# Latent attention scores as row tiles of TensorE, with the projections made for a pair of heads

## Chip, cores, metric

One core of a Trainium2 chip (trn2). The metric is device time in microseconds of one execution of the whole kernel.

## The reference, cut to what matters

A two-layer encoder over 1024 tokens of width 1024, all in fp32. Layer 0 mixes tokens by dilated attention, layer 1 by latent attention with 8 heads; both add 4 heads of attention into a memory of 256 tokens, and end in a mixture of 32 experts. The change is in the latent attention of layer 1:

```python
q = (rms_norm(c_q) @ w_qb).reshape(S, 8, 64 + 32)        # c_q: (1024, 256)
q_nope, q_pe = q[..., :64], apply_rope(q[..., 64:])
kv = (rms_norm(c_kv) @ w_kvb).reshape(S, 8, 64 + 64)      # c_kv: (1024, 128)
k_nope, v = kv[..., :64], kv[..., 64:]
k_pe = apply_rope(k_rope)                                 # (1024, 32), one for all heads
s = (q_nope . k_nope + q_pe . k_pe) * 96 ** -0.5          # per head, 1024 x 1024
o = softmax(s) @ v
```

So a score is a dot product over 96 numbers: 64 unrotated ones and 32 rotated ones, whose key part is the same for every head.

## The kernel before, in words

Every engine has its own program, written out by hand, and semaphores tie them together. The stages stand in the same order on each: layer 0's projections and attentions, its output projection, routing and experts, then for layer 1 the latents, the latent attention, the memory attention, output projection, routing and experts. Weights of the experts stream through a ring of six buffers of 16 KB per partition; the latent attention keeps its queries, keys and weights in the same ring, so SP asks for the second layer's first expert weights only when the latent attention is over (`expert_phase`, line 597).

Latent attention works in 32 units: 4 pairs of heads times 8 tiles of 128 queries. Before it, `latent_projection` (line 1156) makes the values of all heads (`for_act`, copied out by ACT at line 1293), and DVE rotates the shared key part (`latent_norms`, line 1951) into rows 64 to 95 of each of four key buffers. The first two heads are projected ahead of the loop (`head_projection`, line 1176): per head two halves of 512 tokens for the queries, 96 output rows, two products over the 256 latents each, and two products for the keys, 64 output rows, the two halves side by side in the columns of the array. All of them go to bank 7. ACT copies the 64 unrotated rows (`head_copy`, line 1461), DVE rotates the other 32 in four operations (`head_rope`, line 1963, lines 1971 to 1977), and PE waits for both before it writes the bank again. The heads of the next pair are projected inside the loop, one piece per unit: pieces 0 and 1 are query halves, 2 is the key product, 3 only a copy; 8 pieces in the 8 units of a pair.

In the loop PE does, per unit u: scores of head 0 of unit u + 1 (line 1210, banks 0 and 1), the transposes of head 1's probabilities of unit u (`turn`, line 1219), the transpose of the reciprocals of the sums (line 1236), a piece of projection, scores of head 1 of unit u + 1 (banks 2 and 3), the values of unit u (line 1230, both heads side by side in the columns), and the transposes of head 0's probabilities of unit u + 1. A product over fp32 is two instructions on PE. DVE does the maximum over 1024 scores (line 1989), scales it (1991), copies half of the transposed probabilities (1996), makes reciprocals of the sums spread over 128 columns (2005), copies them when they are transposed (2010), rotates a projected half, and multiplies the output (2016). ACT does the exponentials (1482), the other half of the transposed probabilities (1489), and the copies of projections (1468).

The waits that order this: scores of head hd wait until the same head's exponential of the unit before is done, since they write its banks; the values wait for the transposed probabilities and for the copy of the reciprocals; the first scores of a pair wait for the pair's copies and ropes.

The weights of a head are loaded by SP in two small transfers (`head_weights`, line 665), the first two heads' early, the others' when the projections of earlier heads are done. The weights of the output projection, 3 MB, are asked for when the input projection of layer 1 has been read (line 676).

Memory attention, after it, already takes its scores with 64 rows of the array for each head (line 907), two heads at a time:

```python
rows = slice(DH * (h % 2), DH * (h % 2) + DH)
last = mm(ps[:, 2 * b + h % 2, ...], queries[rows, h // 2, ...], keys[rows, h // 2, ...])
```

The experts use the array in columns (line 1051): products for 32 tokens in four column quarters, for 64 tokens in two column halves.

## Time and profile before

| | |
|---|---|
| runs shown | 2440.29, 2444.55, 2451.59 us |
| median | 2444.55 us |
| profiled execution, its own time | 2438.25 us |
| its span, first to last instruction | 2436.1 us |
| instructions in it | 37961 |
| mean granted TensorE clock | 0.946 |

The span leaves 2.15 us of the profiled execution's time outside. Times in the rows are microseconds from the start of the span. Engines: PE is TensorE (PEld its weight loads), DVE is VectorE, ACT is ScalarE, POOL is GpSimd, SP issues DMAs. A matrix instruction is shown from its start to a modelled end, so the distance between two starts says what one costs in a stream. A granted clock of 1.00 is 2.4 GHz, and the other level is 1.2 GHz.

### The profile page before, as it was taken

What the parts mean: (1) busy time and instruction counts of PE and PEld (TensorE: products, weight loads), DVE (VectorE), ACT (ScalarE), POOL (GpSimd) and SP (SyncE); (2) the same over time, 40 slices, a digit from 0 to 9 for tenths busy, and PEclk for the clock granted to TensorE, in tenths of its full rate; (3) what the DMA queues carried; (4) which work ended last, traced back from release to release, by engine and by line L of the source; (5) the groups of instructions that cost most, each with busy time, mean ns of one, the idle gap of its engine ahead of it and who ended that gap; (6) DMA issues with size and microseconds to landing.
All of it is one profiled execution on the core that took longest, in us unless ns stands there. A gap on an engine that the chain in (4) does not pass through costs nothing. (4 is left out here: it accounts for less than half of the span.)

```text
span 2436.1 us, 37961 instructions
## 1 busy us (share of the span) xinstructions
PE 2222.6 (91%) x15351; PEld 1184.0 (49%) x15351; DVE 841.7 (35%) x1791; ACT 468.2 (19%) x943; POOL 343.0 (14%) x401
## 2 busy tenths in 40 slices
PE   8999998886999999998797999989689999999964
PEld 4665757553444444444443556665444444444422
DVE  2133324634121212122825767642422212121216
ACT  0030304221010101011333444431201101010011
POOL 0000000141111111131600000003211111111305
PEclk9999998987999999999897999999689999999997
DMA  9022104344999999997310000010469999999945
GB/s 352 1 76 98 40 1 142 141 184 165 396 391 388 394 386 389 389 387 274 119 52 7 3 5 1 1 70 35 200 224 395 388 400 384 386 378 391 375 158 207
DMA packets 98871, 534.47 MB, mean 219 GB/s; under 512 B 23040, under 2 KB 46880, under 8 KB 73824
## 3 DMA queue, kind: packets, MB, share of 16 engines
q1 hardware_dynamic: 80672, 491.28, 51.8%
q0 software_dynamic: 18112, 41.99, 4.8%
q8 instruction: 60, 0.98, 0.2%
q14 instruction: 27, 0.22, 0.0%
HBM read 510.16 MB, written 41.45 MB: 226 GB/s over the span
## 5 line engine op out<-in xcount | busy, mean ns | idle before, releaser
L825 PE MATMUL banks<-ring,arena 128*32 128x256 f32 (+3 forms) x9952 | 1303.4, 461 | 38.5 <-DMA ring<-in_exp_w_gu 15.0
L825 PEld LDWEIGHTS banks<-ring,arena 128*32 128x32 f32 (+2 forms) x9952 | 536.4, 124 | 746.3 <-issue 608.7
L825 PE MATMUL banks<-ring 128*128 128x512 f32 (+2 forms) x976 | 372.2, 531 | 10.7 <-ACT ring L1468 7.1
L825 PEld LDWEIGHTS banks<-ring 128*128 128x128 f32 (+1 forms) x976 | 183.9, 194 | 156.6 <-issue 139.8
L1830 DVE TENSOR_TENSOR arena<-arena,banks 128x384 f32<-128x384 f32 x65 | 36.0, 554 | 609.7 <-ACT arena L1392 609.7
L761 POOL DMA_INDIRECT expert_out<-arena,scatter_idx x64 | 61.1, 955 | 824.4 <-DVE arena L1839 804.4
L1392 ACT ACTIVATE arena<-banks 128x384 f32<-128x384 f32 x65 | 31.9, 490 | 735.8 <-PE banks L825 735.8
L825 PE MATMUL banks<-arena 128*64 128x128 f32 (+5 forms) x1664 | 157.8, 303 | 16.7 <-DMA arena<-in_mem_w_kv 9.6
L825 PEld LDWEIGHTS banks<-arena 128*64 128x64 f32 (+3 forms) x1664 | 139.0, 169 | 50.2 <-issue 38.0
L718 POOL TENSOR_TENSOR arena<-arena,ln_gb 128x1024 f32<-128x1024 f32 x28 | 69.5, 2482 | 626.5 <-ACT arena L1357 626.5
L1836 DVE COPY arena<-banks 32x256 f32<-32x256 f32 x132 | 56.2, 425 | 280.1 <-PE banks L825 279.2
L825 PE MATMUL banks<-arena,ring 128*128 128x256 f32 (+3 forms) x288 | 101.0, 529 | 13.6 <-DVE ring L1977 11.7
L1407 ACT COPY arena<-banks 32x256 f32<-32x256 f32 x128 | 46.2, 361 | 313.7 <-PE banks L825 313.0
L1600 DVE CUSTOM_DVE_ANT_0 arena<-banks,arena 128x256 f32<-128x256 f32 (+1 forms) x160 | 54.1, 394 | 148.8 <-PE banks L825 145.5
L1989 DVE TENSOR_REDUCE max_and_sum<-banks 128x1 f32<-128x1024 f32 x64 | 77.5, 1212 | 38.6 <-PE banks L825 38.2
L1482 ACT ACTIVATE arena<-banks,neg_max 128x1024 f32<-128x1024 f32 x64 | 71.3, 1114 | 91.7 <-DVE neg_max L1991 90.5
L1031 PEld LDWEIGHTS banks<-ident,arena 96*128 96x128 f32 x520 | 47.5, 146 | 66.3 <-issue 63.4
L1357 ACT ACTIVATE arena<-arena,ln_rstd 128x1024 f32<-128x1024 f32 x32 | 39.7, 1240 | 191.2 <-DVE ln_rstd L1683 191.2
L1031 PE MATMUL banks<-ident,arena 96*128 96x96 f32 x520 | 59.7, 260 | 16.6 <-issue 8.5
L825 PEld LDWEIGHTS banks<-arena,ring 128*128 128x128 f32 (+2 forms) x288 | 48.6, 183 | 51.7 <-issue 47.0
L720 POOL TENSOR_TENSOR arena<-arena,ln_gb 128x1024 f32<-128x1024 f32 x28 | 71.1, 2539 | 2.2
L1826 DVE COPY arena<-banks 128x768 f32<-128x768 f32 x65 | 62.3, 958 | 24.9 <-PE banks L1031 17.5
(176 smaller groups left out, 1575.7 us busy)
## 6 DMA issues: line engine op xcount, KB each, us to landing
ring<-in_exp_w_gu SPq DMA_DIRECT2D x130, 2048.0 KB, 17.2
ring<-in_exp_w_down SPq DMA_DIRECT2D x65, 2048.0 KB, 21.8
ring<-in_x_t SPq DMA_DIRECT2D x6, 2304.0 KB, 16.4
moe_in<-arena POOLq DMA_DIRECT2D x16, 512.0 KB, 3.0
arena<-expert_out SPq DMA_DIRECT2D x16, 512.0 KB, 4.3
ring<-expert_out SPq DMA_DIRECT2D x16, 512.0 KB, 4.4
ring<-in_a_w_in SPq DMA_DIRECT2D x6, 1024.0 KB, 17.3
arena<-in_a_w_in SPq DMA_DIRECT2D x4, 1024.0 KB, 14.0
```

The source lines that it names most:

```text
L718: nc.gpsimd.tensor_tensor(X[:, t], X[:, t], ln_gb[:, 0], ALU.mult).then_inc(gmul_done, 1)
L720: nc.gpsimd.tensor_tensor(X[:, t], X[:, t], ln_gb[:, 1], ALU.add).then_inc(x_ready, 1)
L761: pool.indirect_dma_start(y_d[l][:, :], bass.IndirectOffsetOnAxis(ap=s_idx[0:CAP, b:b + 1], axis=0), ys[0:CAP, b], None, bounds_check=2 * ...
L825: return nc.tensor.matmul(out, lhsT, rhs, start=start, stop=stop)
L1031: last = nc.tensor.transpose(ps[:, k // 4, (k % 4) * CAP:(k % 4 + 1) * CAP], xs[0:CAP, b, k * P:(k + 1) * P], ident[0:CAP, 0:CAP])
L1357: nc.scalar.activation(X[:, t], X[:, t], ACT.Identity, bias=rstd[:, t, 1:2], scale=rstd[:, t, 0:1]).then_inc(norm_done, 1)
L1407: nc.scalar.copy(ys[WIDE:CAP, b, g * 256:(g + 1) * 256], ps[NARROW * g:NARROW * g + NARROW, 7, 0:256])
L1482: nc.scalar.activation(prob[:, hd], ps[:, 2 * hd:2 * hd + 2].rearrange("p a b -> p (a b)"), ACT.Exp, bias=neg_max[:, hd, 0:1], scale=SCALE ...
L1600: last = nc.vector.tensor_tensor_reduce(out=prob[:, b, h * 256:h * 256 + w], in0=ps[:, 2 * b + h % 2, (h // 2) * 256:(h // 2) * 256 + w], ...
L1826: return V.tensor_copy(xs_t[b].rearrange("p (a c) n -> p a (c n)", a=2), ps[:, 0:2, 0:4 * CAP])
L1836: return V.tensor_copy(ys[WIDE:CAP, b, g * 256:(g + 1) * 256], ps[NARROW * g:NARROW * g + NARROW, 7, 0:256])
L1989: V.tensor_reduce(stat[:, hd, 0, 0:1], ps[:, 2 * hd:2 * hd + 2].rearrange("p a b -> p (a b)"), AX.X, ALU.max).then_inc(row_max, 1)
```

## The change

A product over 64 or 32 rows of the array leaves the other rows free, and a row tile is a product put on a part of the rows. The queries and keys are stored anew for that. `q_nope` and `k_nope` hold a pair of heads, one in partitions 0 to 63, one in 64 to 127. `q_rope` holds the rotated part of both heads of a pair, each twice, in four quarters of 32 partitions; `k_rope` holds the rotated key part in four quarters, keys 0 to 511 in the first and third, 512 to 1023 in the second and fourth. A unit's scores are then four products over 64 rows, alternating between the halves, and four over 32 rows, one in each quarter, that add to the same four banks. They are written for both heads at once, at the place of head 0's, and wait until both exponentials of the unit before are done.

The projections are made for the pair: six per pair instead of eight pieces per two heads, each 128 output rows wide (rotated queries, unrotated queries and keys, for each half of the tokens), ten products in all. The first pair's go to banks 0 to 5 without a wait between them, the later ones to bank 7 in the first six units of a pair. DVE rotates two of the six over all 128 partitions, ACT copies the other four. The rope table is stored for all 128 partitions. In DVE's program the rope stands behind the second maximum, in ACT's the copy behind the second exponential. The reciprocal is taken of the two sums, and a copy spreads it. The weights of all heads are loaded in three transfers: the key weights early, the two of the query weights, 512 KB each and stored in the order they are used, behind the wait that the output weights have. The loop of per-head loads on SP is gone.

```diff
-        q_heads = [ring_at(kb, S) for kb in (32, 36, 56, 60)]
-        k_heads = [ring_at(kb, S) for kb in (40, 44, 88, 92)]
-        w_q_head = ring_at(48, 2, 2, QKB)
-        w_k_head = ring_at(49.5, 2, DH)
+        q_nope = ring_at(32, 2, S)
+        k_nope = ring_at(40, 2, S)
+        k_rope = ring_at(48, HALF)
+        q_rope = ring_at(56, 2, S)
+        w_q_nope = ring_at(88, 2, MLA_H, DH)
+        w_q_rope = ring_at(92, 2, MLA_H, 2, ROPE_B)
...
+        PROJ_FOR_DVE = (True, False, False, True, False, False)
+
+        def proj_bank(m, i):
+            return ps[:, i if m == 0 else 7]
+
+        def proj_before(m, i, dve):
+            return (2 if dve else 4) * m + sum(f == dve for f in PROJ_FOR_DVE[:i])
...
-            sp.dma_start(rope_b[DH:QKB], io["rope_b"].rearrange("c p n -> p c n")).then_inc(b_in, 16)
+            sp.dma_start(rope_b, io["rope_b"].rearrange("c p n -> p c n")).then_inc(b_in, 16)
...
-            def head_weights(h, hb, first):
-                if not first:
-                    sp.wait_ge(head_ps, 4 * h - 4)
-                fence(sp)
-                sp.dma_start(w_q_head[:, hb], io["b_w_qb"][0].rearrange("(k p) n -> p k n", p=P)[:, :, bass.ds(h * QKB, QKB)]).then_inc(hw_in[hb], 16)
-                sp.dma_start(w_k_head[:, hb], io["b_w_kvb"][0][:, bass.ds(h * 2 * DH, DH)]).then_inc(hw_in[hb], 16)
-
-            head_weights(0, 0, True)
-            head_weights(1, 1, True)
+            sp.dma_start(w_k_nope[:], io["b_w_kvb"][0].rearrange("p (h c) -> p h c", c=2 * DH)[:, :, 0:DH]).then_inc(hw_in, 16)
             gb_loads(2, ("ln_mix_g", "ln_mix_b"), 1)
             router_loads(1)
             sp.wait_ge(act_full, PC["B"][0] + TT + 4)
+            sp.dma_start(w_q_nope, io["w_q_nope"]).then_inc(hw_in, 16)
+            sp.dma_start(w_q_rope, io["w_q_rope"]).then_inc(hw_in, 16)
             sp.dma_start(w_out[1], io["b_w_out"][0].rearrange("(k p) n -> p k n", p=P)).then_inc(wout_in, 16)
-            with sp.Fori(0, MLA_H // 2 - 1) as i:
-                head_weights(2 * i + 2, 0, False)
-                head_weights(2 * i + 3, 1, False)
...
-            def head_projection(h, j):
-                hb = h % 2
-                if j == 0:
-                    pe.wait_ge(hw_in[hb], 16 * h + 32 - 16 * hb)
-                if j < 3 and h + j > 0:
-                    pe.wait_ge(head_act, 4 * h + j)
-                    pe.wait_ge(head_dve, 2 * h + min(j, 2))
-                cols = slice((j % 2) * HALF, (j % 2 + 1) * HALF)
-                if j < 2:
+            def pair_projection(m, i):
+                if m == 0 and i == 0:
+                    pe.wait_ge(hw_in, 48)
+                if m > 0:
+                    pe.wait_ge(head_act, proj_before(m, i, False))
+                    pe.wait_ge(head_dve, proj_before(m, i, True))
+                cols = slice(i // 3 * HALF, (i // 3 + 1) * HALF)
+                out = proj_bank(m, i)
+                if i % 3 == 2:
+                    last = mm(out, w_k_nope[:, 2 * m:2 * m + 2].rearrange("p h c -> p (h c)"), ckv_t[:, cols])
+                else:
                     for k in range(2):
-                        last = mm(ps[0:QKB, 7, :], w_q_head[:, hb, k], cq_t[:, k, cols], k == 0, k == 1)
-                    last.then_inc(head_ps, 1)
-                elif j == 2:
-                    for half in range(2):
-                        mm(ps[half * DH:(half + 1) * DH, 7, :], w_k_head[:, hb],
-                           ckv_t[:, half * HALF:(half + 1) * HALF]).then_inc(head_ps, 1)
+                        if i % 3 == 0:
+                            w = w_q_rope[:, k, 2 * m:2 * m + 2].rearrange("p h r c -> p (h r c)")
+                        else:
+                            w = w_q_nope[:, k, 2 * m:2 * m + 2].rearrange("p h c -> p (h c)")
+                        last = mm(out, w, cq_t[:, k, cols], k == 0, k == 1)
+                last.then_inc(head_ps, 1)
...
             def latent_attention():
                 u0 = unit0[(1, "mla")]
                 pe.wait_ge(act_free, PC["B"][0] + 20)
                 pe.wait_ge(k_rot_done, 1)
-                for h in range(2):
-                    for j in range(4):
-                        head_projection(h, j)
-
-                def score(u, hd):
+                for i in range(6):
+                    pair_projection(0, i)
+
+                def score(u):
                     m, t = divmod(u, TT)
-                    h = 2 * m + hd
                     if t == 0:
-                        pe.wait_ge(head_act, 4 * h + 4)
-                        pe.wait_ge(head_dve, 2 * h + 2)
+                        pe.wait_ge(head_act, 4 * m + 4)
+                        pe.wait_ge(head_dve, 2 * m + 2)
                     if u > 0:
-                        pe.wait_ge(probs, u0 + 2 * u + hd - 1)
+                        pe.wait_ge(probs, u0 + 2 * u)
+                    queries = slice(t * P, (t + 1) * P)
                     for c in range(2):
-                        last = mm(ps[:, 2 * hd + c], q_heads[h % 4][0:QKB, t * P:(t + 1) * P], k_heads[h % 4][0:QKB, c * HALF:(c + 1) * HALF])
-                    last.then_inc(scores, 1)
+                        for hd in range(2):
+                            rows = slice(DH * hd, DH * hd + DH)
+                            mm(ps[:, 2 * hd + c], q_nope[rows, m % 2, queries], k_nope[rows, m % 2, c * HALF:(c + 1) * HALF], True, False)
+                    for hd in range(2):
+                        for c in range(2):
+                            r = ROPE_B * (2 * hd + c)
+                            last = mm(ps[:, 2 * hd + c], q_rope[r:r + ROPE_B, m % 2, queries], k_rope[r:r + ROPE_B], False, True)
+                        last.then_inc(scores, 1)
...
-                score(0, 0)
-                score(0, 1)
+                score(0)
                 turn(0, 0)
                 for u in range(PAIR_UNITS):
                     more = u + 1 < PAIR_UNITS
                     if more:
-                        score(u + 1, 0)
+                        score(u + 1)
                     turn(u, 1)
                     reciprocals(u)
                     m, t = divmod(u, TT)
-                    if m + 1 < MLA_H // 2:
-                        head_projection(2 * m + 2 + t // 4, t % 4)
-                    if more:
-                        score(u + 1, 1)
+                    if m + 1 < MLA_H // 2 and t < 6:
+                        pair_projection(m + 1, t)
...
-            def head_copy(h, j):
-
-                act.wait_ge(head_ps, 4 * h + j + 1)
-                if h >= 4:
-                    act.wait_ge(scores, unit0[(1, "mla")] + 2 * TT * (h // 2 - 1))
-                dst = (q_heads if j < 2 else k_heads)[h % 4][0:DH, (j % 2) * HALF:(j % 2 + 1) * HALF]
-                half = j - 2 if j > 2 else 0
-                nc.scalar.copy(dst, ps[half * DH:(half + 1) * DH, 7]).then_inc(head_act, 1)
+            def pair_copy(m, i):
+
+                act.wait_ge(head_ps, 6 * m + i + 1)
+                if m >= 2:
+                    act.wait_ge(scores, unit0[(1, "mla")] + 2 * TT * (m - 1))
+                dst = (k_nope if i % 3 == 2 else q_nope)[:, m % 2, i // 3 * HALF:(i // 3 + 1) * HALF]
+                nc.scalar.copy(dst, proj_bank(m, i)).then_inc(head_act, 1)
...
                         exponentials(u + 1, 0)
+                        exponentials(u + 1, 1)
                     m, t = divmod(u, TT)
-                    if m + 1 < MLA_H // 2:
-                        head_copy(2 * m + 2 + t // 4, t % 4)
+                    if m + 1 < MLA_H // 2 and t < 6 and not PROJ_FOR_DVE[t]:
+                        pair_copy(m + 1, t)
                     if more:
-                        exponentials(u + 1, 1)
                         turned(u + 1, 0)
...
-                    for keys in k_heads:
-                        last = V.tensor_tensor(keys[rows, cols], rope_tmp_b[rows, 0], rope_tmp_b[rows, 1], ALU.add)
+                    for r in (ROPE_B * h, DH + ROPE_B * h):
+                        last = V.tensor_tensor(k_rope[r:r + ROPE_B], rope_tmp_b[rows, 0], rope_tmp_b[rows, 1], ALU.add)
...
-            def head_rope(h, j):
+            def pair_rope(m, j):
 
                 V = nc.vector
-                rows, cols = slice(DH, QKB), slice(j * HALF, (j + 1) * HALF)
-                n = 2 * h + j + 1
-                dve.wait_ge(head_ps, 4 * h + j + 1)
-                if h >= 4:
-                    dve.wait_ge(scores, unit0[(1, "mla")] + 2 * TT * (h // 2 - 1))
-                V.stream_shuffle(rope_tmp_b[rows, 0], ps[rows, 7], swap_b).then_inc(hr_a, 1)
-                V.tensor_tensor(rope_tmp_b[rows, 1], ps[rows, 7], rope_b[rows, 0, cols], ALU.mult).then_inc(hr_b, 1)
+                cols = slice(j * HALF, (j + 1) * HALF)
+                n = 2 * m + j + 1
+                bank = proj_bank(m, 3 * j)
+                dve.wait_ge(head_ps, 6 * m + 3 * j + 1)
+                if m >= 2:
+                    dve.wait_ge(scores, unit0[(1, "mla")] + 2 * TT * (m - 1))
+                if n > 1:
+                    dve.wait_ge(head_dve, n - 1)
+                V.stream_shuffle(rope_tmp_b[:, 0], bank, swap_b).then_inc(hr_a, 1)
+                V.tensor_tensor(rope_tmp_b[:, 1], bank, rope_b[:, 0, cols], ALU.mult).then_inc(hr_b, 1)
                 dve.wait_ge(hr_a, n)
-                V.tensor_tensor(rope_tmp_b[rows, 0], rope_tmp_b[rows, 0], rope_b[rows, 1, cols], ALU.mult).then_inc(hr_c, 1)
+                V.tensor_tensor(rope_tmp_b[:, 0], rope_tmp_b[:, 0], rope_b[:, 1, cols], ALU.mult).then_inc(hr_c, 1)
                 dve.wait_ge(hr_b, n)
                 dve.wait_ge(hr_c, n)
-                V.tensor_tensor(q_heads[h % 4][rows, cols], rope_tmp_b[rows, 0], rope_tmp_b[rows, 1], ALU.add).then_inc(head_dve, 1)
+                V.tensor_tensor(q_rope[:, m % 2, cols], rope_tmp_b[:, 0], rope_tmp_b[:, 1], ALU.add).then_inc(head_dve, 1)
...
-                    V.reciprocal(recip_wide[:], stat[:, :, 1, 0:1].to_broadcast([P, 2, DH])).then_inc(den_ready, 2)
+                    V.reciprocal(recip_den[:, 0, 0:2], stat[:, :, 1, 0]).then_inc(recip_step, 1)
+                    dve.wait_ge(recip_step, u + 1)
+                    V.tensor_copy(recip_wide[:], recip_den[:, 0, 0:2].rearrange("p (h a) -> p h a", a=1).to_broadcast([P, 2, DH])).then_inc(den_ready, 2)
                     if more:
                         maximum(u + 1, 0)
                     turned(u, 1)
                     dve.wait_ge(recip_ps, u + 1)
                     V.tensor_copy(recip_t[:], ps[:, 6, P:2 * P]).then_inc(recip_kept, 1)
-                    if m + 1 < MLA_H // 2 and t % 4 < 2:
-                        head_rope(2 * m + 2 + t // 4, t % 4)
                     if more:
                         maximum(u + 1, 1)
+                    if m + 1 < MLA_H // 2 and t in (0, 3):
+                        pair_rope(m + 1, t // 3)
...
-        "rope_b": rope_table(ROPE_B, ROPE_B, 1, np.arange(S)),
+        "rope_b": rope_table(ROPE_B, ROPE_B, 4, np.arange(S)),
...
+    w_qb = np.asarray(inputs["b_w_qb"])[0].reshape(2, P, MLA_H, QKB).transpose(1, 0, 2, 3)
+    a["w_q_nope"] = np.ascontiguousarray(w_qb[..., :DH])
+    a["w_q_rope"] = np.ascontiguousarray(np.repeat(w_qb[..., None, DH:], 2, axis=3))
```

## Rows read from the trace of the kernel before

**Rows 1.** The page: engine busy over the span, DMA busy by slice.

```profile
...
PE 2222.6 (91%) x15351; PEld 1184.0 (49%) x15351; DVE 841.7 (35%) x1791; ACT 468.2 (19%) x943; POOL 343.0 (14%) x401
...
DMA  9022104344999999997310000010469999999945
```

**Rows 2.** Windows; columns: stretch, length, busy of PE, PEld, DVE, ACT, POOL, clock, DMA.

```profile
...
1277.00:1309.00 32.00, 19.05 (x28) 5.16 (x29) 10.44 (x20) 5.92 (x9) 0.00 (x0) 0.63 0.04 9
```

**Rows 3.** Timeline, stage start; columns: start, length, engine, line, operation, idle before it.

```profile
...
1277.03 1.96 PE L825 MATMUL banks<-arena,ring 128*96 128x512 f32 x4 [0.68 <-ACT arena L1293]
...
1279.06 0.72 DVE L1971 STREAM_SHUFFLE ring<-banks 32x512 f32<-32x512 f32 x1
...
1281.20 0.68 DVE L1977 TENSOR_TENSOR ring<-ring 32x512 f32<-32x512 f32 x1
...
1306.15 7.06 PE L825 MATMUL banks<-ring 96*128 96x512 f32 x8
...
1309.97 1.23 DVE L1989 TENSOR_REDUCE max_and_sum<-banks 128x1 f32<-128x1024 f32 x1 [5.87 <-PE banks L825]
...
1312.68 0.18 PEld L1219 LDWEIGHTS banks<-ident,arena 128*128 128x128 f32 x1 [0.90 <-ACT arena L1482]
...
1313.92 1.88 PE L825 MATMUL banks<-ring 96*128 96x512 f32 x4
```

**Rows 4.** Timeline of three units inside a pair of heads.

```profile
...
1332.90 1.88 PE L825 MATMUL banks<-ring 96*128 96x512 f32 x4
...
1341.45 1.88 PE L825 MATMUL banks<-ring 96*128 96x512 f32 x4
...
1343.17 1.04 PE L1219 MATMUL banks<-ident,arena 128*128 128x128 f32 x8
...
1343.37 1.23 DVE L1989 TENSOR_REDUCE max_and_sum<-banks 128x1 f32<-128x1024 f32 x1 [0.17 <-PE banks L825]
...
1344.70 0.69 DVE L1996 COPY arena<-banks 128x512 f32<-128x512 f32 x1
...
1345.31 0.28 DVE L2010 COPY recip_t<-banks 128x128 f32<-128x128 f32 x1
...
1345.96 1.97 PE L825 MATMUL banks<-arena 128*64 128x128 f32 x32
...
1347.86 1.09 PE L1219 MATMUL banks<-ident,arena 128*128 128x128 f32 x8
...
1348.79 1.88 PE L825 MATMUL banks<-ring 96*128 96x512 f32 x4
...
1357.85 1.88 PE L825 MATMUL banks<-ring 96*128 96x512 f32 x4
```

**Rows 5.** Timeline: a pair's first unit, and the last unit's first scores.

```profile
...
1380.69 3.31 PE L825 MATMUL banks<-ring 96*128 96x512 f32 x4 [2.36 <-ACT ring L1468]
...
1577.32 1.88 PE L825 MATMUL banks<-ring 96*128 96x512 f32 x4
```

**Rows 6.** Timeline of PE in the memory attention behind the stage.

```profile
...
1602.65 1.90 PE L825 MATMUL banks<-mem_values,arena 128*128 128x65 f32 x16
...
1604.48 1.14 PE L825 MATMUL banks<-mem_keys_t,arena 64*128 64x256 f32 x8
...
1605.55 1.09 PE L919 MATMUL banks<-ident,arena 128*128 128x128 f32 x8
```

**Rows 7.** Chain of waits: one expert's down projection.

```profile
...
2361.90 5.54 PE banks L825 x48
```

**Rows 8.** Timeline of the last unit: the reciprocals' copy and the values.

```profile
...
1587.42 0.28 DVE L2010 COPY recip_t<-banks 128x128 f32<-128x128 f32 x1
...
1587.85 1.97 PE L825 MATMUL banks<-arena 128*64 128x128 f32 x32 [0.96 <-DVE recip_t L2010]
```

**Rows 9.** SP's queue (timeline), and DMA issues: KB, us to landing.

```profile
...
1256.18 0.38 SPq L677 DMA_DIRECT2D ring<-in_b_w_out  x1
...
ring<-in_b_w_out SPq DMA_DIRECT2D x1, 3072.0 KB, 10.4
```

More of the change, by code:

```diff
@@ L107, in build @@
         recip_t = sb("recip_t", [P, P])
+        w_k_nope = sb("w_k_nope", [P, MLA_H, DH])
         merge_e = sb("merge_e", [P, TT, NG, GH])
@@ L224, in build @@
         den_ready = sem("den_ready")
+        recip_step = sem("recip_step")
         recip_ps = sem("recip_transposed")
@@ L286, in build @@
         b_in = sem("layer_b_in")
-        hw_in = [sem("head_weights_in0"), sem("head_weights_in1")]
+        hw_in = sem("head_weights_in")
         head_ps = sem("head_ps")
@@ L1459, in latent_norms @@
                     copy_out(v_b[:, t])
-            def head_copy(h, j):
-                act.wait_ge(head_ps, 4 * h + j + 1)
-                if h >= 4:
-                    act.wait_ge(scores, unit0[(1, "mla")] + 2 * TT * (h // 2 - 1))
-                dst = (q_heads if j < 2 else k_heads)[h % 4][0:DH, (j % 2) * HALF:(j % 2 + 1) * HALF]
-                half = j - 2 if j > 2 else 0
-                nc.scalar.copy(dst, ps[half * DH:(half + 1) * DH, 7]).then_inc(head_act, 1)
+            def pair_copy(m, i):
[4 more added lines that the diff above has]
+                nc.scalar.copy(dst, proj_bank(m, i)).then_inc(head_act, 1)
             def latent_attention():
                 u0 = unit0[(1, "mla")]
-                for h in range(2):
-                    for j in range(4):
-                        head_copy(h, j)
+                for i in range(6):
+                    if not PROJ_FOR_DVE[i]:
+                        pair_copy(0, i)
                 def exponentials(u, hd):
@@ L1981, in latent_attention @@
                 V = nc.vector
-                for h in range(2):
-                    for j in range(2):
-                        head_rope(h, j)
+                for j in range(2):
+                    pair_rope(0, j)
                 def maximum(u, hd):
@@ L2100, in constants @@
         "rope_a": np.stack([rope_table(DH // 4, DH, 2, group_order(g)) for g in range(NG)]),
-        "rope_b": rope_table(ROPE_B, ROPE_B, 1, np.arange(S)),
+        "rope_b": rope_table(ROPE_B, ROPE_B, 4, np.arange(S)),
         "masks": group_masks(),
     }
-WEIGHTS = ("a_w_in", "a_w_out", "b_w_in", "b_w_qb", "b_w_kvb", "b_w_out", "mem_w_kv", "ln_mix_g", "ln_mix_b",
+WEIGHTS = ("a_w_in", "a_w_out", "b_w_in", "b_w_kvb", "b_w_out", "mem_w_kv", "ln_mix_g", "ln_mix_b",
            "ln_ffn_g", "ln_ffn_b", "router_w_grp", "router_b_grp", "router_w_exp", "router_b_exp")
```

## The prediction

> **What bounds the kernel now.** I read the page first. TensorE (PE) is busy for 91% of the span, and the DMA slices show two long stretches at 9, which are the two layers' experts, fed by weights [rows 1]. Latent attention lies between them, in slices where DMA is at 0 or 1, and the second layer's expert weights are not asked for before it ends: what is saved in this stage therefore moves everything behind it forward, one for one. So I read only this stage closely, in the timeline, from the first projection at 1277.03 to the last values behind 1587.85 [rows 3, 8].
>
> The stage has two parts. **Its start** is poor: eight head projections go through one bank, each waiting for the rope (DVE) and copy (ACT) of the one before. PE is busy 19.05 of 32 us there at a granted clock of 0.63, and the first scores start at 1306.15, themselves at the 1.2 GHz level: eight instructions take 7.06 us, where four take 1.88 later [rows 2, 3]. **The loop** of 32 units is PE back to back: a unit's scores of one head take 1343.17 - 1341.45 = 1.72 us, which is 0.43 per instruction and 0.86 per fp32 product of 512 columns, two instructions each. A unit without a projection takes 7.34 us, with the short key projection 8.55, with half a query projection 9.06 [rows 4]. DVE and ACT fit beside that. At the first unit of each later pair PE waits 2.36 us for ACT's last key copy [rows 5].
>
> **The start, after the change.** The first projection was released by ACT's last V copy, not by the key rope [rows 3], so it starts at 1277.03 as before, and the shorter key rope (two adds instead of four per half) is worth nothing. Six projections with ten products then go to six banks with no wait: 10 x 0.86 = 8.6 us, to 1285.6, at the 2.4 GHz level, since PE came in at it and now has no holes. The second rope follows the seventh product, at 1283.05: 0.3 us until it starts and 2.8 for its four operations [rows 3], 1286.2. On 128 partitions instead of 32 I take the same durations, because the free size is the same. The last copy, priced by DVE's copy of 512 columns, 0.69 [rows 4], ends at 1286.6. Scores start at 1286.7.
>
> From there: the maximum starts 3.10 us after the scores start (below), a second maximum comes 1.33 later (1343.37 to 1344.70 [rows 4]), and from a maximum's start to the first load that its probabilities allow is 2.71 (1309.97 to 1312.68 [rows 3]). 1286.7 + 3.1 + 1.33 + 2.71 = 1293.9. That is when unit 1's scores may start; before it was 1313.92 [rows 3]. **Saved: 20.0 us.** If the clock is at the low level for the first scores, their 2.6 us of streaming doubles: bound 17.4. Nothing in sight gives more than 1 us on top.
>
> **The scores themselves.** Removed per unit: four products of 96 rows, 4 x 0.86 = 3.44. Added: four of 64 rows in two row halves and four of 32 rows in quarters. That halves stream together is in the trace: eight instructions of 256 columns in memory attention take 1605.55 - 1604.48 = 1.07; one after another they would be 8 x 0.215 = 1.72, in pairs 0.86 [rows 6]. The 0.21 over is the first weight load and the way out of the tile shape; the way in costs about 0.12 (16 short instructions took 1.83 [rows 6], against 16 x 0.107). Quarters of rows are nowhere in the trace. Their bounds are all four at once, 0.86, and one after another, 3.44. The nearest row is the experts' down projection: 32 instructions of 256 columns in column quarters and 16 of 512 in halves take 5.54; four at a time and two at a time that is 1.72 + 3.44 = 5.16, with quarters only in pairs 6.88 [rows 7]. So I take 0.86, plus 0.21.
>
> From start of scores to the transposes: 1.72 + 0.21 + 0.86 + 0.21 = 3.00, against 3.44, with another 0.12 on the way in: 0.32 us gained per unit, not the 0.86 that the streaming alone promises. The rule that speaks against the change is in the Trainium skill, "TensorEngine Tiling (Array Packing)", Tiling Modes: changing the tiling mode drains the engine. The trace agrees with it, by the 0.1 to 0.2 us at each change of shape.
>
> **The new wait.** Both heads' scores now stand together in front of the unit, where the second head's used to stand between the reciprocals' transposition and the values. They were the cover for this chain: scores end, maximum, copy of the transposed probabilities, copy of the reciprocals, values. Its pieces: 0.20 from the scores' end to the maximum, 1.94 from there to the reciprocals' copy (1343.37 to 1345.31) [rows 4], 0.43 from there to the values (1587.42 to 1587.85) [rows 8]. With S the start of the scores, the last slot ends at S + 2.90, the maximum starts at S + 3.10, the values can't start before S + 5.47. PE itself would be there at 3.00 + 0.93 (transposes, as 1347.86 to 1348.79) + 0.11 (one instruction of 128 columns) + projection + 0.10 for the change of shape: at S + 5.86 with a projection of two products, 5.00 with one, 4.14 with none. So it waits 0, 0.47 and 1.33 us. Behind the values' start come 1.90 for them, 0.93 for transposes [rows 4] and 0.12: a unit is 8.81 us with two products and 8.42 otherwise.
>
> Whether the next scores are held by the second exponential, which they now need: the second maximum starts at S + 5.33, its probabilities are there 2.71 later, S + 8.04, below 8.42. Not held, but with 0.4 us to spare only.
>
> **Sum of the loop,** from unit 1's scores to unit 31's, 30 steps. Before: 1577.32 - 1313.92 = 263.4 [rows 3, 5]. Three pairs at 4 x 9.06 + 2 x 8.55 + 2 x 7.34 = 68.0, and 6 x 7.34, give 248.1; the remaining 15.3 are mostly the three pair boundaries, the 2.36 us of waiting and the slow clock behind it (four instructions in 3.31 [rows 5]). After: six projections per pair at the first six of eight units, so the copies are two units old when the next pair starts and this wait goes. 12 units at 8.81 and 18 at 8.42 = 257.3. **Saved: 6.1**, made of -15.3 (boundaries), -3.0 (12 x 0.25), -0.8 (6 x 0.13), +13.0 (12 units at 1.08 more). In the last unit the same wait costs 5.47 + 1.90 - (7.34 - 0.93) = **1.0** more.
>
> **At nothing:** The reciprocal of 128 columns becomes one of two and a copy; it is done in the 2 us in which DVE waits for the scores. The rope of a pair, 2.8 us in units 0 and 3, now stands before the output's multiplication: DVE ends it at S + 9.6, copies the transposed half of the next unit by S + 10.7, and the PE needs that at S + 8.8 + 3.0 = 11.8. Cover 1.1 us; without it six units would lose what is over. The query weights can no longer be loaded early, since they lie on the input weights: they are asked for where the output weights were, 1256.18, ahead of them; 1 MB of 3 MB that took 10.4 us [rows 9] is a few us against 20 until 1277. The per-head loads go. SP's queue has nothing else that is due in the stage.
>
> **Sum:** 20.0 + 6.1 - 1.0 = 25.1 us. The profiled execution took 2438.25 and would take 2413; the median of the three runs is 2444.55, 6.3 above it, so the forecast is 2444.55 - 25.1 = 2419.4, **2419**.
>
> **Rivals.** *Slower: the row quarters stream one after another.* Place: the second half of every unit's scores; price 3.44 - 0.86 = 2.58 us x 32 = 83 us, on PE's chain and on the maximum's; 2502. It decides from 0.78 us per unit on, about two at a time. For it: no row shows four row tiles, and each writes all 128 output columns to a bank of its own. Against: rows 6 and 7. Chance 0.06. *In pairs:* 0.86 x 32 = 27.5, which eats the gain: 2447, chance 0.08. *Partly:* the four tiles' weights are loaded one after another before the last can stream, three more loads at 0.1 to 0.18 [rows 3], 0.3 to 0.5 us x 32 = 10 to 17: 2429 to 2436, chance 0.17. The Trainium skill, "TensorE: Matmul & The Clock Gate", Part 3, gives 3.07 times for four row tiles instead of four; by that the rope products take 1.12 instead of 0.86, 8.4 us in all, and the time would be 2428. *The clock:* the new holes of 1.3 us, or the one at the start, bring the low level: a stretch like that behind the boundary costs 2 to 3 us; four of them make 2429. Against: PE stays busy for over 80% of each unit. Chance 0.09. *Better:* the changes of shape are hidden or the chain to the values is shorter by 0.3: 0.3 x 30 = 9, 2410. Chance 0.08. *The forecast:* 0.52.
>
> About 0.5%, 12 us, is what a measurement of this kernel can tell from no change. Faster by more: the forecast, better, clock and most of partly, 0.83; within: pairs and the rest, 0.11; slower 0.06. The range leaves out the two serial cases and takes in the low bound of the start: 2407 to 2438.
>
> **What would show it.** First scores at about 1286.7 instead of 1306.15 and unit 1's at 1294; no wait for ACT's projection copy at pair starts; per unit about 3.0 us from the first 64-row product to the transposes, with the 32-row group at 1.07; an idle of 1.3 us before the values, released by the reciprocals' copy, in units without projection. A 32-row group near 2 or 3.6 us makes the forecast wrong; so does a unit bound by the second exponential, or a clock under 0.9 in the loop.

## The result, and the profile after

The changed kernel takes **2415.56 us** (median of 4 runs, 2412.38 to 2422.12) against 2442.93 for the kernel before (4 runs): ratio **0.9894, 95% interval 0.9876 to 0.9912**. The forecast was 2419, its range 2407 to 2438. The profiled execution took 2414.21 us (before 2438.25), its span is 2411.9 (before 2436.1).

The page of the changed kernel, engine busy and DMA slices, as in [rows 1]:

```profile
PE 2192.0 (91%) x15591; PEld 1169.7 (48%) x15591; DVE 797.4 (33%) x1779; ACT 457.8 (19%) x927; POOL 344.1 (14%) x401
...
DMA  9013103444999999997510000011479999999945
```

PE has 240 instructions more and is busy 30.6 us less; its share of the span is the same. Only the latent attention changed: from its first projection to the memory attention's first scores it took 312.7 us before and takes 1563.98 - 1277.58 = 286.4. It began 0.55 us later, and what lies behind it took 1.5 us longer; 26.3 - 0.55 - 1.5 is the 24.2 us of the spans. The end of the stage and the work behind it, timeline of PE before and then of the changed kernel:

```profile
1589.74 2.00 PE L825 MATMUL banks<-mem_keys_t,arena 64*128 64x256 f32 x16
...
1594.53 1.09 PE L919 MATMUL banks<-ident,arena 128*128 128x128 f32 x8 [2.79 <-ACT arena L1337]
```

```profile
1550.62 3.06 PE L827 MATMUL banks<-ring 64*128 64x512 f32 x16
...
1563.98 2.00 PE L827 MATMUL banks<-mem_keys_t,arena 64*128 64x256 f32 x16
1568.78 1.97 PE L921 MATMUL banks<-ident,arena 128*128 128x128 f32 x8 [2.80 <-ACT arena L1343]
```

The memory attention's first transposes take 1.97 us where they took 1.09, which is the low clock level, and 15 us behind the stage the changed kernel is 1.8 us late by this. The second profile of the changed kernel, shown below, has the same 1.97 there. Why the clock fell at that place was not tried.

The start of the stage in the timeline of the changed kernel, PE, ACT and DVE together, as in [rows 3]:

```profile
1277.58 3.70 PE L827 MATMUL banks<-arena,ring 128*128 128x512 f32 x8 [0.68 <-ACT arena L1299]
...
1287.11 3.06 PE L827 MATMUL banks<-ring 64*128 64x512 f32 x16 [0.68 <-ACT ring L1473]
...
1290.20 1.22 DVE L1996 TENSOR_REDUCE max_and_sum<-banks 128x1 f32<-128x1024 f32 x1 [3.60 <-PE banks L827]
...
1294.22 3.06 PE L827 MATMUL banks<-ring 64*128 64x512 f32 x16 [0.22 <-ACT arena L1487]
```

The first scores start 9.53 us after the first projection, where they took 29.1 [rows 3], and their sixteen instructions run at the full clock. Unit 1's scores follow at 1294.22.

The loop, timeline of PE of the changed kernel, units with two projection products, with a single one and with none, as in [rows 4]:

```profile
1301.96 1.09 PE L1228 MATMUL banks<-ident,arena 128*128 128x128 f32 x8
1302.98 3.06 PE L827 MATMUL banks<-ring 64*128 64x512 f32 x16
1305.97 1.09 PE L1228 MATMUL banks<-ident,arena 128*128 128x128 f32 x8
...
1307.01 1.88 PE L827 MATMUL banks<-arena,ring 128*128 128x512 f32 x4
1308.82 1.97 PE L827 MATMUL banks<-arena 128*64 128x128 f32 x32
...
1311.74 3.06 PE L827 MATMUL banks<-ring 64*128 64x512 f32 x16
...
1337.65 3.06 PE L827 MATMUL banks<-ring 64*128 64x512 f32 x16
...
1343.11 1.97 PE L827 MATMUL banks<-arena 128*64 128x128 f32 x32 [0.41 <-DVE recip_t L2019]
...
1346.03 3.06 PE L827 MATMUL banks<-ring 64*128 64x512 f32 x16
...
1351.49 1.97 PE L827 MATMUL banks<-arena 128*64 128x128 f32 x32 [1.27 <-DVE recip_t L2019]
...
1354.41 3.06 PE L827 MATMUL banks<-ring 64*128 64x512 f32 x16
...
1362.80 3.06 PE L827 MATMUL banks<-ring 64*128 64x512 f32 x16
```

One PE row stands for halves and quarters together; where the quarters begin is seen in the timeline's weight loads:

```profile
1304.90 0.31 PEld L827 LDWEIGHTS banks<-ring 32*128 32x128 f32 x8 [0.76 <-issue]
```

The three kinds of unit are 8.76, 8.38 and 8.38 us long. The pair boundary at 1354.41 has no wait, and the unit behind it is 8.39, where the first scores of a pair waited 2.36 us [rows 5]. In place of that wait stands a new one, 1.27 us before the values, put down to DVE's copy of the transposed reciprocals. What that copy waited for is in DVE's timeline of the same unit:

```profile
1349.12 1.22 DVE L1996 TENSOR_REDUCE max_and_sum<-banks 128x1 f32<-128x1024 f32 x1 [1.89 <-PE banks L827]
...
1350.46 0.69 DVE L2003 COPY arena<-banks 128x512 f32<-128x512 f32 x1
...
1351.07 0.28 DVE L2019 COPY recip_t<-banks 128x128 f32<-128x128 f32 x1
```

DVE idles 1.89 us until the scores end, then takes the maximum and copies the transposed probabilities and the transposed reciprocals, while PE has nothing left to do. By groups of instructions, PE from 1275 to 1565 (busy, mean ns | idle before, releaser):

```profile
L827 PE MATMUL banks<-ring 64*128 64x512 f32 x256 | 63.6, 615 | 0.9 <-ACT ring L1473 0.7 <-ACT arena L1487 0.2
L827 PE MATMUL banks<-arena 128*64 128x128 f32 x1024 | 63.0, 275 | 20.4 <-DVE recip_t L2019 20.4
L827 PE MATMUL banks<-ring 32*128 32x512 f32 x256 | 36.5, 640 | 0.0
```

That wait, in the second of these lines, is 20.4 us in all. So a stage that gained 26.3 us holds 20.4 us of new idle time, and the question for the experiments is what the row tiles themselves bring.

### The profile page after: what moved, and what is told of

Read it like the earlier page. It is cut to its first block and busy times, and to the rows that moved or that the text cites. A ratio compares the mean times of both kernels' runs of the same rounds, so it can differ in the third digit from the quotient of the medians.

```text
span 2411.9 us, 38329 instructions
## 1 busy us (share of the span) xinstructions
PE 2192.0 (91%) x15591; PEld 1169.7 (48%) x15591; DVE 797.4 (33%) x1779; ACT 457.8 (19%) x927; POOL 344.1 (14%) x401
## 5 line engine op out<-in xcount | busy, mean ns | idle before, releaser
L827 PE MATMUL banks<-ring 128*128 128x512 f32 (+3 forms) x1232 | 339.9, 550 | 5.6 <-issue 4.0
L827 PEld LDWEIGHTS banks<-ring 128*128 128x128 f32 (+2 forms) x1232 | 168.5, 188 | 149.4 <-issue 138.8
L827 PE MATMUL banks<-arena 128*64 128x128 f32 (+5 forms) x1664 | 155.4, 299 | 36.2 <-DVE recip_t L2019 20.4
L827 PE MATMUL banks<-arena,ring 128*128 128x256 f32 (+1 forms) x256 | 85.6, 486 | 0.7 <-ACT arena L1299 0.7
L1228 PE MATMUL banks<-ident,arena 128*128 128x128 f32 x512 | 69.9, 279 | 3.6 <-ACT arena L1487 2.7
L1228 PEld LDWEIGHTS banks<-ident,arena 128*128 128x128 f32 x512 | 54.8, 141 | 33.5 <-issue 29.9
## 6 DMA issues: line engine op xcount, KB each, us to landing
arena<-in_a_w_in SPq DMA_DIRECT2D x4, 1024.0 KB, 13.5
```

Source lines behind the costliest of these rows:

```text
L827: return nc.tensor.matmul(out, lhsT, rhs, start=start, stop=stop)
L1228: last = nc.tensor.transpose(ps[:, 4 + c // 4, (c % 4) * P:(c % 4 + 1) * P], prob[:, hd, c * P:(c + 1) * P], ident[:])
```

## The experiments

Stage times below are: first projection to the transposition of unit 0's reciprocals ("start", 40.35 before, 20.56 after), from there to unit 31's ("loop", 269.23 before, 262.71 after), and the whole stage. The loop here begins and ends elsewhere than the prediction's.

**The tiles taken away** (the changed kernel with the scores of a head as two full-height products; the rotated part is left out, and the unrotated products of both heads are added up):

```diff
-                    for c in range(2):
-                        for hd in range(2):
-                            rows = slice(DH * hd, DH * hd + DH)
-                            mm(ps[:, 2 * hd + c], q_nope[rows, m % 2, queries], k_nope[rows, m % 2, c * HALF:(c + 1) * HALF], True, False)
                     for hd in range(2):
                         for c in range(2):
-                            r = ROPE_B * (2 * hd + c)
-                            last = mm(ps[:, 2 * hd + c], q_rope[r:r + ROPE_B, m % 2, queries], k_rope[r:r + ROPE_B], False, True)
+                            last = mm(ps[:, 2 * hd + c], q_nope[:, m % 2, queries], k_nope[:, m % 2, c * HALF:(c + 1) * HALF])
```

> The changed kernel without row tiles: a unit's scores are four products over all 128 rows of the array, at the same place and under the same waits; the rotated part is left out and the two heads' unrotated products are added up. My theory: the tiles save what they stream less (0.86 us a unit) minus the changes of shape. Scores to transposes become 3.44 instead of 2.99, with 0.12 less on the way in: units with two projection products 9.07 instead of 8.76, the others 8.84 instead of 8.39, about 12 us more than the changed kernel in all, near 2427. Rival, the changes of shape eat all of it: no change, 2415. Rival, streaming alone counts: 0.86 x 32 = 27 more, 2443.

2415.92 us (4 runs), ratio 0.9897 [0.9873, 0.9921]: the whole times show no difference from the kernel with the tiles. The stage does, in the profiles: start 20.38, loop 265.40, stage 290.44, which is 4.0 us longer. Of these, 2.7 are loop and 1.5 the last unit's values, which took 3.49 us instead of 1.97 at the low clock level. Units with two products are 9.06 us, which is 0.30 more and as expected; the others are 8.37 and not 8.84, which is the miss. Timeline of this kernel, a unit without projection:

```profile
1346.51 3.60 PE L827 MATMUL banks<-ring 128*128 128x512 f32 x8
...
1348.42 1.23 DVE L1991 TENSOR_REDUCE max_and_sum<-banks 128x1 f32<-128x1024 f32 x1 [0.62 <-PE banks L827]
...
1352.05 1.97 PE L827 MATMUL banks<-arena 128*64 128x128 f32 x32 [0.97 <-DVE recip_t L2014]
...
1354.88 3.60 PE L827 MATMUL banks<-ring 128*128 128x512 f32 x8
```

The scores take 3.43 us on PE instead of 2.99, but head 0's are finished half-way, so the first maximum starts 1.91 us after the scores start instead of 3.09. The values start at S + 5.54 against S + 5.46: here the transposes that end later and the copies of what they made are the chain, there the maximum. Row tiles finish all four banks together, and in the units without that much other work for PE, what they save on PE they give back by starting DVE later. Their whole worth is 2.7 us of loop: 12 x 0.30 in the units with two products, less 0.9 in the others.

**All rotated products in one row quarter:**

```diff
-                            r = ROPE_B * (2 * hd + c)
+                            r = 0
```

> The changed kernel with all four rotated products of a unit in the first row quarter, which gives head 0's rotated part on the first half of the keys to all four banks. My theory, quarters stream side by side and now must not: the group of eight 32-row instructions takes 8 x 0.43 + 0.21 = 3.65 us instead of 1.07, every unit is 2.6 longer, all in all 83 us more, near 2498. Rival, the four never overlapped fully: less than that by what they overlap less; if they went in pairs, 1.7 a unit and 55 us.

2528.49 us (one run), stage 396.43. PE's timeline, one unit with a single and one with two products at full clock, and the beginning of a slow one:

```profile
1324.78 5.61 PE L827 MATMUL banks<-ring 64*128 64x512 f32 x16
1330.32 1.09 PE L1228 MATMUL banks<-ident,arena 128*128 128x128 f32 x8
...
1335.41 5.61 PE L827 MATMUL banks<-ring 64*128 64x512 f32 x16
...
1346.72 5.67 PE L827 MATMUL banks<-ring 64*128 64x512 f32 x16
1352.33 1.97 PE L1228 MATMUL banks<-ident,arena 128*128 128x128 f32 x8
```

From scores to transposes it is 5.54 us instead of 2.99: the eight instructions of the rotated part now follow one another at 0.43 us each, and cost 2.55 more. So in the changed kernel the four quarters do stream together. A full-clock unit is 10.63 with one product and 11.31 with two, that is 2.25 and 2.55 longer, about as expected. The 30 us over the expectation were not foreseen. Most units are longer than these two, up to 13.03 us, with instructions at the low clock level, as in the last line; more on this at the end.

**The start put back to one bank:**

```diff
-            return ps[:, i if m == 0 else 7]
+            return ps[:, 7]
...
-                if m > 0:
+                if m > 0 or i > 0:
```

> The changed kernel with the first pair's six projections all in bank 7, each waiting for the copy or rope of the one before. My theory, the start's gain is the missing waits and the clock they cost: two waits of 3.3 us for ropes and three of about 1.1 for copies, and products at the low clock behind them. First scores 19 to 28 us behind the first projection instead of 9.5, about 14 us more in all, near 2430. Rival, the start gained by having fewer products and instructions: at most 3 us more.

2430.78 us (10 runs), ratio 0.9956 [0.9941, 0.9970]. PE's timeline:

```profile
1275.32 1.98 PE L827 MATMUL banks<-arena,ring 128*128 128x512 f32 x4 [0.68 <-ACT arena L1299]
1280.18 1.96 PE L827 MATMUL banks<-arena,ring 128*128 128x512 f32 x4 [2.88 <-DVE ring L1985]
...
1289.47 3.65 PE L827 MATMUL banks<-arena,ring 128*128 128x512 f32 x4 [2.88 <-DVE ring L1985]
...
1295.60 3.06 PE L827 MATMUL banks<-ring 64*128 64x512 f32 x16 [0.68 <-ACT ring L1473]
```

Scores start 20.3 us after the first projection instead of 9.5; the start is 32.96 instead of 20.56, the loop is the same at 262.74. The medians are 15.2 us apart, as expected; the profiled execution, at 2421.68 us the fastest of the ten, has 12.4 of it. The first scores come 10.8 us later by this count, of which the two waits of 2.88 for the rope are the largest part. A projection at the low clock level (3.65 us instead of 1.96) adds 1.7, and unit 1's scores, slow in part, another 1.6.

**The reciprocals' copy moved to ACT,** behind its copy of the probabilities:

```diff
+                    act.wait_ge(recip_ps, u + 1)
+                    nc.scalar.copy(recip_t[:], ps[:, 6, P:2 * P]).then_inc(recip_kept, 1)
...
-                    dve.wait_ge(recip_ps, u + 1)
-                    V.tensor_copy(recip_t[:], ps[:, 6, P:2 * P]).then_inc(recip_kept, 1)
```

> The changed kernel with the copy of the transposed reciprocals moved from DVE to ACT, which is idle there. My theory, the hole before the values is DVE's chain maximum, probabilities' copy, reciprocals' copy: the values then follow the probabilities' copy, 5.19 instead of 5.46 behind the scores' start, units without or with one product go from 8.39 to 8.1, 18 of them: 5 us less, near 2411. Rival, something else ends just behind it (second exponential, ACT's own queue): no change or up to 5 us more.

2409.95 us (5 runs), ratio 0.9870 [0.9850, 0.9890]. PE's timeline:

```profile
1345.73 3.06 PE L827 MATMUL banks<-ring 64*128 64x512 f32 x16
...
1350.95 1.97 PE L827 MATMUL banks<-arena 128*64 128x128 f32 x32 [1.03 <-DVE arena L2005]
...
1353.88 3.06 PE L827 MATMUL banks<-ring 64*128 64x512 f32 x16
```

The unit is 8.14 instead of 8.38, the loop 257.77, the stage 281.33: the chain was as supposed, one link shorter gives 5 us of stage. The wait left, 1.03, is for DVE's copy behind the maximum. Relative to the kernel before, this is as fast as anything below.

**Scores behind the projection instead of ahead of the unit,** with DVE's copies ahead of both maxima:

```diff
-                    if more:
-                        score(u + 1)
                     turn(u, 1)
...
                         pair_projection(m + 1, t)
+                    if more:
+                        score(u + 1)
```

> The changed kernel with both heads' scores moved from the front of the unit to just before the values, and both maxima behind DVE's two copies. My theory: the hole before the values goes, but the next exponentials become the bound: from the scores' start to the second probabilities 3.1 + 1.33 + 2.71 = 7.1 us, then transposes, reciprocals and the projection stand in line behind them. Units about 8.4 without a projection, 9.3 with one product, 10.2 with two: 16 to 23 us more than the changed kernel, near 2435. Rival, only the hole counts: 13 us less.

2489.99 us (one run), stage 362.6. PE's timeline:

```profile
1310.03 1.94 PE L1228 MATMUL banks<-ident,arena 128*128 128x128 f32 x8 [2.54 <-DVE arena L2003]
...
1322.62 1.07 PE L1228 MATMUL banks<-ident,arena 128*128 128x128 f32 x8 [1.24 <-ACT arena L1494]
```

A miss by 55 us. The two groups of transposes now stand back to back and write the same banks, so the second waits for the copies of what the first made. In a unit with a rope that copy is queued on DVE behind the rope (2.54), in a unit with a projection's copy it is queued on ACT behind that (1.24). The expectation had PE's order right and had left out what those copies stand behind. With PE busy 80% of 1300 to 1400 the granted clock is 0.91 there, which costs more. With these orders of PE and DVE, the scores in front of the unit are therefore the better of the two places: they cover those copies.

**Projections one unit later,** in units 1 to 6 of a pair:

```diff
-                    if m + 1 < MLA_H // 2 and t < 6:
-                        pair_projection(m + 1, t)
+                    if m + 1 < MLA_H // 2 and 1 <= t < 7:
+                        pair_projection(m + 1, t - 1)
```

> The changed kernel with the six projections of a pair in its units 1 to 6 instead of 0 to 5, so that ACT's last copy stands right before the next pair's first scores. My theory, the wait at the pair boundary is the distance of that copy from the scores, and ACT ends it at about S + 8.7 where the scores could start at S + 8.4: a wait of 0.3 to 0.6 us at three boundaries, 1 to 2 us in all. Rival, the boundary cost before was not the copy: no change at all. Second rival: the wait alone makes the clock fall again, 4 to 5 us a boundary.

2417.90 us (one run), stage 286.47 against 286.40: no change, and the expected 1 to 2 us did not come. Timelines of ACT and of PE at the boundary:

```profile
1357.94 0.57 ACT L1473 COPY ring<-banks 128x512 f32<-128x512 f32 x1
```

```profile
1357.53 1.09 PE L1228 MATMUL banks<-ident,arena 128*128 128x128 f32 x8
1358.57 3.06 PE L827 MATMUL banks<-ring 64*128 64x512 f32 x16
```

The last copy ends at 1358.51 and the scores that need it start at 1358.57, 1.04 behind the transposes where it is 1.02 elsewhere. One unit of room is just enough, two are not needed. This run alone does not say what the boundary cost before, since it made no wait; the next one does.

**The kernel before, with ACT's copy of the last key half moved one unit forward:**

```diff
-                        head_copy(2 * m + 2 + t // 4, t % 4)
+                        for j in {2: (2, 3), 3: ()}.get(t % 4, (t % 4,)):
+                            head_copy(2 * m + 2 + t // 4, j)
```

> The kernel before with one edit on ACT: the copy of the second half of the keys stands with that of the first, one unit earlier, so the next pair's scores find it done. My theory, the boundary cost 4.3 to 5.9 us three times for this copy alone: unit 1's to unit 31's scores 249 instead of 263.4, 14 us less than before, near 2429. Rival, the boundary is bound by something else (bank 7, the ropes): less than 5 us.

2426.94 us (6 runs), ratio 0.9944 [0.9925, 0.9962]. PE's timeline at a boundary, for [rows 5]:

```profile
1372.70 1.88 PE L825 MATMUL banks<-ring 96*128 96x512 f32 x4
...
1375.30 0.27 PE L1236 MATMUL banks<-ident,recip_wide 128*128 128x128 f32 x1
1375.41 1.88 PE L825 MATMUL banks<-ring 96*128 96x512 f32 x4
...
1380.05 1.88 PE L825 MATMUL banks<-ring 96*128 96x512 f32 x4
```

The scores at 1375.41 are those that waited 2.36 us at 1380.69 [rows 5]; they stand right behind the reciprocals' transposition. The unit is 7.35 us where the three units at boundaries took 11.61, 13.22 and 11.61, and the loop is 254.84, 14.4 less than before. Half of the 14.4 is the three waits of 2.36; the other half is instructions at the low clock level behind them. The key half had been ready a unit earlier all along; only its copy was late.

**The kernel before, with the first two heads' projections in six banks** (made after the kernel with both edits, which stands below):

```diff
+        def head_bank(h, j):
+            return 3 * h + min(j, 2) if h < 2 else 7
...
-                if j < 3 and h + j > 0:
+                if j < 3 and h > 1:
...
+                if n > 1:
+                    dve.wait_ge(head_dve, n - 1)
```

(with `head_bank(h, j)` for bank 7 in the projections, copies and ropes).

> The kernel before with only the start mended: the first two heads' projections in six banks. Theory, start and boundaries add up: the run with both took 33 us off and the one with the boundaries alone 14.6, so the start alone takes 18 to 19: 2423 to 2424, and the boundary waits of 2.36 us stay. Rival, the two share a cause (the clock): less than 15.

2421.23 us (6 runs), ratio 0.9927 [0.9912, 0.9941]: 18.6 us, as expected. Start 21.82. The three units at the boundaries, with their wait of 2.36, take 9.97, 11.61 and 13.21 us here: the same wait costs 2.6 to 5.9 us, by what the clock does behind it.

**Both of these in the kernel before:**

> The kernel before with that edit and with the first two heads' projections in six banks without a wait; scores over the full array, in two places per unit, as before. My theory, most of the gain has nothing to do with row tiles: start 19 us less, boundaries 14 less, 33 in all, and no hole before the values: 2409, 6 us below the changed kernel. Rival, the ropes of the first two heads (four of 2.85 us on DVE, one after another) hold the start at 14 us from the first projection to the second head's scores: 3 us worse, 2412.

**2408.58 us** (4 runs, 2407.85 to 2410.12), ratio 0.9872 [0.9850, 0.9894], the lowest median of all, though the ratio of the kernel with the reciprocals' copy on ACT, 0.9870, is no higher. Start 20.51, loop 254.83, stage 278.47, the shortest. The second head's first scores wait 2.27 us for a rope, 13.5 us behind the first projection, as the rival had it, but the start is 19.8 us shorter all the same. Windows of this kernel and then of the changed one (length; busy of PE, PEld, DVE, ACT, POOL; clock; DMA):

```profile
1320.00:1560.00 240.00, 237.22 (x1754) 151.78 (x1753) 183.84 (x320) 112.35 (x193) 0.00 (x0) 1.00 0.02 5
```

```profile
1320.00:1560.00 240.00, 220.15 (x1873) 135.79 (x1872) 146.06 (x308) 103.05 (x180) 0.00 (x0) 1.00 0.01 1
```

Both have the full clock; PE is busy 99% here and 92% there. The wait before the values, 20.4 us in the changed kernel, is 1.0 here.

**The changed kernel once more:**

> The changed kernel unchanged, beside the next one and the kernel before on one chip. Theory: 0.989 of before, near 2416. Rival, the earlier comparison held a difference between chips or loads: outside 0.985 to 0.993.

2417.81 us (5 runs, 2411.96 to 2419.64), ratio 0.9899 [0.9884, 0.9914], stage 287.76. Its loop is the same, 262.72, but its start is 21.91 instead of 20.56: the first transposes took 1.89 us instead of 1.10, at the low clock level. The stage with the two small edits is thus 8 to 9 us shorter than the changed kernel's, in both of its profiles. The intervals of the ratios overlap, so the advantage in whole time rests on the stage times and on medians 7 and 9 us apart, of runs that were not made side by side.

## Why the prediction was right

**The start, "saved: 20.0 us": right.** From the first projection to unit 1's scores it was 36.89 us and is 16.64, which is 20.2; the first scores were to start 9.67 us behind the first projection and did so at 9.53. In the second profile it is 17.15, and the start is 1.4 us longer by its end, with instructions at the low clock level; that the first profile has none there is luck, of less than the 2.6 us that the prediction's bound left for it. Six banks in the kernel before shorten its start by 18.5, nearly the same, so the banks are enough without the pair; the pair with one bank takes 7.4 off.

**The tiles, "0.32 us gained per unit": right in size.** From scores to transposes it is 2.99 (3.00), and 1.02 from transposes to scores where it was 0.93 [rows 4]. A unit with two products gains 0.30 by this, as the kernel without tiles shows. The group of quarters takes 1305.97 - 1304.90 = 1.07, as forecast; one after another the same eight instructions made it 2.55 longer, 3.62, in the experiment. Of the rivals, "one after another", "in pairs" and "partly" fall by this row: two at a time would be 1.93, three more weight loads 1.4 to 1.6. The Trainium skill, "TensorE: Matmul & The Clock Gate", Part 3, has 3.07 times for four row tiles; by it the group would be 1.33, and the measurement, which is 1.07 with the change of shape in it, decides against it here. The Trainium skill, "TensorEngine Tiling (Array Packing)", Tiling Modes, has the engine drain when the mode changes; the trace agrees, with 1304.90 - 1302.98 = 1.92 for 1.72 of streaming, and 0.21 over in the quarters.

**The new wait, "0, 0.47 and 1.33 us": right,** 0, 0.41 and 1.27. With S the start of a unit's scores, the maximum starts at S + 3.09 (3.10), the values at S + 5.46 (5.47). Moved to ACT, the last link gives its 0.24 back, as the mechanism wants.

**The loop, "saved: 6.1": 7.0.** From unit 1's scores to unit 31's it is 1550.62 - 1294.22 = 256.4, for 257.3. The units are 8.76 and 8.38 (8.81 and 8.42). In the prediction's four terms: -15.3, -3.6 (12 x 0.30), -1.0 (6 x 0.17), +12.5 (12 x 1.04), and 0.4 more in a single late unit. The term for the boundaries is shown: taking their wait away gives 14.4 in the kernel before. The other 0.9 lies at the beginning of that kernel's loop: from unit 1's scores to the transposition of the reciprocals it takes 1317.38 - 1313.92 = 3.46 us, where it takes 1344.04 - 1341.45 = 2.59 further on. PE waits 0.67 of it for ACT's copy behind the second exponential, which was late after the slow scores of the start.

**The last unit, "1.0 more": 0.94** (1563.98 - 1550.62 = 13.36, against 12.42).

**What was costed at nothing** was nothing. The second exponential never held the scores inside the loop; it holds unit 1's only, on the path that the start was worked out from. The rope behind the second maximum ends 9.3 us after S and the copy behind it at S + 10.1, for 9.6 and 10.7. The query weights, asked for at 1259.56, took 3.7 and 4.6 us. The clock rival did not come in the loop: 1.00 from 1320 to 1560, in both profiles.

So 20.2 + 7.0 - 0.9 = 26.3, for 25.1. The median fell by 27.4, and the forecast is 3.4 us above it; of this 1.2 is the stage, the rest that the runs of before have a median 1.6 lower than the three shown, and the spread of both. In the repeat the medians are 22.0 us apart, so a hit to within 3.4 us is partly luck.

What the prediction did not say is which of these gains needed the change. Of 27 us the start brings about 20 and the boundaries 14, and each can be had in the kernel before with a few lines. Against that stand 1.04 us in each of 12 units for both heads' scores in front. The tiles, the part that gives the change its name, save 0.30 us in 12 units. Not tried was the changed kernel with the second head's scores put back between the reciprocals' transposition and the values, which would show whether the pair's projections are worth keeping.

## What to carry to other kernels

Before an operation is made shorter, look at who takes its result: work that ends in one piece at 3.0 us can be worth no more than the same work that ends in two pieces at 1.7 and 3.4, if the next engine's chain begins with the first piece. When a rewrite gains, undo its parts one by one in the new kernel and do them one by one in the old: here the place of one copy and six bank numbers took off more than the whole change, and the old loop with them was the shorter one, 254.8 us against 262.7. A wait at a seam that comes once in eight units is cheap to mend if the data have long been there and only a copy stands at the wrong place in its engine's order.

## What the hardware showed

With the rotated products all in one row quarter, the granted clock fell although PE hardly ever idled. Windows of that kernel, columns as above:

```profile
1300.00:1400.00 100.00, 98.07 (x544) 57.14 (x543) 43.56 (x90) 29.75 (x52) 0.00 (x0) 0.88 0.00 1
1400.00:1500.00 100.00, 98.07 (x557) 56.38 (x556) 45.40 (x93) 30.18 (x53) 0.00 (x0) 0.91 0.00 1
```

A busy share of 98% has 0.88 and 0.91 here, and 92% has 1.00 in the changed kernel. The stretches differ in that for 3.6 us of each unit only a quarter of the array's rows is at work. Whether this is the cause was not tried by itself, and it is a single run. The only other kernel below 0.95 in the loop, at 0.91, is the one with PE busy 80%.

A change between row halves, row quarters and the full array cost about 0.2 us each time it led out of a tiled shape (1.92 for 1.72 of streaming, 1.07 for 0.86), and 0.1 on the way in (1.02 against 0.93). DVE's four rope operations on 128 partitions (0.73, 0.68, 0.68, 0.69 us) took what they take on 32 [rows 3]. A fp32 product of 512 columns was 0.86 us whether it had 32 rows (2 x 0.43 in one quarter), 96 (1.72 for two) or 128 (3.43 for four), so rows left empty are lost unless another tile fills them.
